# A hybrid decoder block on one core: second-half placement of the attention's values, the fourth output block summed from PSUM, earlier scale row, spread first loads, shifted mixer instructions

## What is computed

```python
mod = c_act @ w_ada[l] + b_ada[l]
shift, scale, gate = jnp.split(mod, 3, axis=-1)
h = rmsnorm(x, g_pre[l]) * (1.0 + scale[:, None]) + shift[:, None]
p = h @ w_in[l]
(a_in, a_g, b_q, b_f, b_i, b_g, c_x, c_b, c_c, c_g,
 d_q, d_k, d_v, d_g, m_g) = jnp.split(p, IN_OFFSETS, axis=-1)
y_pool = pool_mixer(a_in, pool_w[l], pool_scale[l]) * jax.nn.silu(a_g)
y_hgrn = hgrn2_mixer(b_q, b_f, b_i, lower_bounds[l], hgrn_norm[l]) * jax.nn.silu(b_g)
y_conv = short_conv_mixer(c_x, c_b, c_c, conv_w[l]) * jax.nn.silu(c_g)
y_diff = diff_attention(d_q, d_k, d_v, diff_lam[l], diff_norm[l], l) * jax.nn.silu(d_g)
gates = jax.nn.sigmoid(m_g.reshape(B_, T, N_BRANCH, D))
merged = (gates[:, :, 0] * (y_pool @ w_merge_pool[l]) + ...)
out = merged @ w_out[l]
x = x + gate[:, None] * rmsnorm(out, g_post[l])
```

## Time and profile before

| | us |
|---|---|
| median of 3 runs | 2758.57 (2758.25 to 2764.52) |
| the profiled execution | 2759.86 |
| its span, first to last instruction | 2757.8 |
| of it, PE busy | 2355.1 |

### The profile page before, as it was taken

One profiled execution on the slowest core, in us unless ns is written; L12 is line 12 of the kernel. 1 busy time (PEld: TensorE's weight loads), 2 busy tenths in 40 slices (PEclk: granted clock), 3 DMA queues, 4 the chain that ended last, 5 costly groups with the idle time before them and its releaser, 6 DMA issues. The chain is left out here.

```text
span 2757.8 us, 35490 instructions
## 1 busy us (share of the span) xinstructions
PE 2355.1 (85%) x11572; PEld 1913.1 (69%) x11572; DVE 1773.7 (64%) x2868; ACT 1240.0 (45%) x2613; POOL 1231.3 (45%) x1015
## 2 busy tenths in 40 slices
PE   3698868778988889996899999998898965798898
PEld 3576656667776678785787777777677754677676
DVE  6775554544989896544777776688899734453442
ACT  3553444434443444543565656553444333243342
POOL 1442322222866665532333433465767605352543
PEclk9899988989999999998999999999999987899999
DMA  5357533323434334545342332143333356485772
GB/s 209 111 186 228 145 105 90 102 72 116 126 101 122 103 97 128 174 132 151 83 119 77 98 96 83 60 134 117 107 110 123 96 171 159 120 231 143 193 198 73
DMA packets 327262, 350.84 MB, mean 127 GB/s; under 512 B 26416, under 2 KB 244912, under 8 KB 326064
## 3 DMA queue, kind: packets, MB, share of 16 engines
q1 hardware_dynamic: 327088, 348.67, 42.8%
HBM read 242.15 MB, written 106.43 MB: 126 GB/s over the span
## 5 line engine op out<-in xcount | busy, mean ns | idle before, releaser
L1603 PE MATMUL gb<-h_hi,w_hi 128*128 128x512 f32 x1904 | 804.2, 422 | 83.7 <-DVE o L1199 53.4
L1604 PE MATMUL gb<-h_lo,w_hi 128*128 128x512 f32 x1904 | 766.9, 403 | 0.0
L1605 PE MATMUL gb<-h_hi,w_lo 128*128 128x512 f32 x1904 | 766.5, 403 | 0.0
L1191 DVE TENSOR_TENSOR w_lo<-w,w_hi 128x512 fp32r<-128x512 f32 x340 | 333.8, 984 | 337.3 <-ACT w_hi L900 336.5
L1603 PEld LDWEIGHTS gb<-h_hi,w_hi 128*128 128x128 f32 x1904 | 375.0, 197 | 173.7 <-issue 95.9
L1605 PEld LDWEIGHTS gb<-h_hi,w_lo 128*128 128x128 f32 x1904 | 372.4, 196 | 84.1
L1604 PEld LDWEIGHTS gb<-h_lo,w_hi 128*128 128x128 f32 x1904 | 375.4, 197 | 69.8 <-issue 0.2
L916 ACT ACTIVATE o<-gb 128x512 f32<-128x512 f32 x340 | 201.7, 593 | 347.8 <-PE gb L1605 300.1
L764 POOL TENSOR_TENSOR C_prob<-C_prob,C_cf 128x512 f32<-128x512 f32 (+3 forms) x160 | 157.8, 1006 | 383.8 <-DVE C_cf L1299 366.8
L989 ACT ACTIVATE C_prob<-C_sc,C_negm 128x512 f32<-128x512 f32 (+3 forms) x320 | 196.9, 620 | 280.9 <-DVE C_negm L1277 275.0
L748 POOL TENSOR_TENSOR o<-o 128x512 f32<-128x512 f32 x68 | 98.0, 1441 | 409.2 <-ACT o L916 409.1
(11 more groups left out here) (227 smaller groups left out, 4312.2 us busy)
## 6 DMA issues: line engine op xcount, KB each, us to landing
w<-in_w_in_dram SPq DMA_DIRECT2D x136, 512.0 KB, 4.1
gT_scratch<-o SPq DMA_DIRECT2D x128, 256.0 KB, 2.7
D_gate<-gT_scratch SPq DMA_DIRECT2D x32, 1024.0 KB, 9.6
pT_scratch<-o SPq DMA_DIRECT2D x80, 256.0 KB, 3.3
C_qt<-qB_scratch SPq DMA_DIRECT2D x128, 128.0 KB, 2.7
C_ks<-kT_scratch SPq DMA_DIRECT2D x48, 256.0 KB, 4.8
A_x_all<-in_x_dram SPq DMA_DIRECT2D x16, 512.0 KB, 6.5
A_ada<-in_w_ada_dram SPq DMA_DIRECT2D x8, 1024.0 KB, 12.1
```

Of the source, the lines that this page charges most:

```text
L1191: tt(w_lo[n % RING][:, :, :], source(n), w_hi[n % RING][:, :, :].bitcast(F32), ALU.subtract).then_inc(wlo, 1)
L1603: mm(to, hi[:, k, :], h_hi[j][:, k, :], start=(fresh and k == 0), stop=False, skip_group_check=True)
L1604: mm(to, hi[:, k, :], h_lo[j][:, k, :], start=False, stop=False, skip_group_check=True)
L1605: last = mm(to, lo[:, k, :], h_hi[j][:, k, :], start=False, stop=(k == KH - 1), skip_group_check=True)
```

## The change

Eight edits in one:

1. In the first half of the tokens PE takes the transpose back, the values and the transposes of a step half a product after its scores (`attention_behind`), and the transpose back one step earlier (7 instead of 8 steps after the unit's end). DVE's `gate_out` stands ahead of the maxima there, and for the second half ahead of the combination. In the second half ACT copies the turned piece between its two exponentials.
2. The product of j = 4 is no longer copied by ACT and added by POOL: DVE adds bank and block 3 into block 2.
3. The units come in the order k, q, v, v, gate, gate, k, q instead of v, v, gate, gate, k, q, k, q. Attention stands in slots 50 to 109 and 284 to 354.
4. The first loads of attention are issued in five parts, one a slot, from 5 slots ahead on.
5. The row of scales is loaded from slot 6 on, one piece in 3 slots, into one buffer, and ends at slot 35.
6. q is kept in another order in DRAM: 2 stores of 128 rows for a block instead of 4 of 64; its loads read pieces of 512 B instead of 2 KB.
7. Mixers: `shares`'s four scalings go from DVE to ACT; POOL's `same_level` is gone, PE reads the last level from `k_s` and `q_s` themselves.
8. Mixers: transposes from 2 to 4, tokens 3 to 5, norms 11 to 12, root 12 to 13, finish 13 to 14, store 14 to 15; in the second half a block in 12.5 slots, from slot 372.

```diff
-PAIR_COLS = (28, 30, 32, 34, 24, 20, 26, 22) + (4, 6, 8, 0, 2, 10, 12, 14, 16, 18) + tuple(range(36, 68, 2))
+PAIR_COLS = (24, 20, 28, 30, 32, 34, 26, 22) + (4, 6, 8, 0, 2, 10, 12, 14, 16, 18) + tuple(range(36, 68, 2))
+COPIED, SUMMED = (0, 2, 3, 6), (1, 4, 5)
-ATTENTION = ((62, 50), (287, 70))
-MIX_BASE = [130 + 12 * i for i in range(8)] + [374 + 12 * i for i in range(8)]
+ATTENTION = ((50, 60), (284, 71))
+MIX_BASE = [130 + 12 * i for i in range(8)] + [372 + 25 * i // 2 for i in range(8)]
-PREP, ROW = 5, 38
+PREP, ROW = 5, 6
...
+                y = 2 * at0 + s * 2 * span // att_steps[half]
+                att_at[divmod(y, 2)] = half, s
+                att_behind[divmod(y + 1 - half, 2)] = half, s
...
             def load_row(k):
-                if k >= 2:
-                    sp.wait_ge(row_used, k - 1)
-                sp.dma_start(row_in[k % 2], ada_v[:, k, 2 * D:3 * D]).then_inc(row_loaded[k % 2], 16)
+                if k:
+                    sp.wait_ge(row_used, k)
+                else:
+                    sp.wait_ge(mod_summed, 1)
+                sp.dma_start(row_in, ada_v[:, k, 2 * D:3 * D]).then_inc(row_loaded, 16)
...
                 for half in range(HALVES):
-                    if n == ATTENTION[half][0] - (5, 4)[half]:
-                        begin_attention(half)
+                    if 0 <= n - ATTENTION[half][0] + 5 < 5:
+                        begin_attention(half, n - ATTENTION[half][0] + 5)
...
-            def cross(u):
-
-                pool.wait_ge(copied, 5 * u + 4)
-                tt(o[2][:, :], o[2][:, :], o[3][:, :], ALU.add).then_inc(crossed, 1)
...
-                b = {1: 0, 5: 1}[j]
+                b, c = {1: (0, 0), 4: (2, 3), 5: (1, 1)}[j]
                 dve.wait_ge(product_done, n + 1)
-                dve.wait_ge(copied, 5 * u + 1 + b)
-                tt(o[b][:, :], gb[n % 2][:, :], o[b][:, :], ALU.add).then_inc(summed, 1)
+                dve.wait_ge(copied, 4 * u + {1: 1, 4: 3, 5: 2}[j])
+                if j == 4:
+                    output_free(u, b)
+                tt(o[b][:, :], gb[n % 2][:, :], o[c][:, :], ALU.add).then_inc(summed, 1)
...
                 a(f_s[:, :, :], in3[i % 2][:, 2:4, :], ACT.Sigmoid)
-                a(k_s[i % 2][:, :, :], in3[i % 2][:, 2:4, :], ACT.Sigmoid, scale=-1.0)
+                link(a(k_s[i % 2][:, :, :], in3[i % 2][:, 2:4, :], ACT.Sigmoid, scale=-1.0))
+                for t in range(2):
+                    a(f_s[:, t, :], f_s[:, t, :], ACT.Identity, scale=omlb[:, t:t + 1], bias=lb[:, t:t + 1])
+                    a(k_s[i % 2][:, t, :], k_s[i % 2][:, t, :], ACT.Copy, scale=omlb[:, t:t + 1])
...
             def shares(i):
                 dve.wait_ge(sig_ready, i + 1)
-                for t in range(2):
-                    ts(k_s[i % 2][:, t, :], k_s[i % 2][:, t, :], omlb[:, t:t + 1], None, ALU.mult)
-                for t in range(2):
-                    ins = ts(f_s[:, t, :], f_s[:, t, :], omlb[:, t:t + 1], lb[:, t:t + 1], ALU.mult, ALU.add)
-                link(ins)
...
+            def attention_behind(half, s):
+                i = None if half else finished(half, s, ON)
+                if i is not None:
+                    turn_back(i)
                 z = piece(half, s, VALUES)
...
-                i = mix_step(n, 11)
+                i = mix_step(n, 12)
                 if i is not None:
                     norms(i)
-                i = mix_step(n, 2)
+                i = mix_step(n, 4)
                 if i is not None:
                     transposes(i)
```

More of the change, by code:

```diff
@@ L1526, in _ @@
                             distances(ending[z])
+                    i = finished(half, s, GATE) if half else None
+                    if i is not None:
+                        gate_out(i)
                     z = piece(half, s, COMBINE)
@@ L1529, in _ @@
                         combine(z)
-                    i = finished(half, s, GATE)
-                    if i is not None:
-                        gate_out(i)
                 for half in range(HALVES):
```

223 lines of the change are left out of this document (113 added, 110 removed).

## The result

| | us |
|---|---|
| median before (4 runs beside it) | 2758.41 (2757.41 to 2764.52) |
| median after (4 runs) | 2598.84 (2593.64 to 2601.82) |
| ratio, with its 95% interval | 0.9415 (0.9395 to 0.9435) |
| profiled execution after, its span | 2601.82, 2600.0 |

A forecast was written before the change was run, and what follows sets the result against it. PE, busy 85% of the span, was taken as the bound, losing time to waits and low clock. Terms -76 - 20 - 15 + 5 - 40 - 2 = -148 took 2759.9 to 2612, so 2611 for the median; range 2575 to 2690.

The forecast's parts named there:

- The signs that it named: Waits, clock and DVE share expected if right, such as first attention's clock 0.95 or more, mixers' DVE under 90%.
- the wait only changes its name: Rival, first half's attention: PE waits for `C_on` as before for `C_y_out`, the 76 us are gone; 2687, chance 0.05.
- the stores stay the bound: Rival where q, k and first loads share a queue: 35 us stay, start costs 10 more; 2656, chance 0.10.
- the better case: Rival: first half's waits and clock loss go entirely and the mixers give 60 us; 2562, chance 0.06.
- The attention's order, -76: First half's attention: -66.6 of waits, -36.7 of clock, +16 at transpose back, +11 small waits; bounds -95 and -40.
- The fourth block, 0 in the attention: DVE gains 68 additions, 46.6 us; hidden outside the mixers, +9.6 us of DVE per half in them.
- the new add hides in its idle time: Outside the mixers, DVE is busy 52 to 72% of the time, so its added fourth-block work was taken as hidden.
- Units, row, first loads, -20 and -15, start +5: Before first attention -20 (-5 to -30); second half's first scores -15 (-8 to -20); start +5 (0 to +15).
- Mixers, -40: Both halves' mixers: lighter DVE and later norms and transposes give -20 a half; bounds 0 and -60 in all.
- The norms come a product later: Mixers: norms move 2.7 to 3.9 us later, against waits for the state of 3.7 mean, 5.4 at most.
- ACT's order in the second half, -2: Second half's attention: values get their input sooner, the second exponential comes later; -2 us, bounds -8 and +8.

The follow-up runs named there:

- the burst in the changed kernel: Changed kernel with the 21 first loads of the second half's attention issued in one slot, 4 ahead, as before: 2605.77 us, ratio 0.9453.
- the root first: Changed kernel with the norms' root (Ln and Exp) ahead of the sigmoids in ACT's slot, not behind them: 2577.54 us, ratio 0.9336.
- two attempts: Changed kernel, root ahead of sigmoids; first half's transpose back ahead of the next step's scores (2577.11 us), or last in its own step (2573.31 us).

## Why the prediction was right, and where it was not

**Sign and size.** -148 forecast, -158 in the profiled executions. The signs that it named came: no wait for `C_y_out`, clock 0.98 in the first attention, 2.7 us for the state, 3.0 us at the second half's first scores, DVE at 85% in the mixers, 60.7 us of waits for DVE's additions. None of the rivals came whole. Of "the wait only changes its name" 25.8 us did, a mean of 0.92, where 0.5 was taken; 2 of the 28 waits passed 2 us. Of "the stores stay the bound" the part on the start did. That the sum came so close is in part luck: the attention's order and the mixers gave 26 and 16 us less than forecast, the start lost 9 more, and the fourth block gave some 33 for which the sum had nothing. Two details don't follow from the working: half the way from 2611 to the better case is 2586, not the range's 2575, and a load of q is 128 KB in the profile, not 64 (its median time to landing went from 2.7 to 2.9 us, so the 512-byte pieces cost little, as was taken).

**The attention's order, -76.** Undoing it gives back 50 us. I counted all of the 66.6 us and all of the clock's 36.7 as this one edit's; with the old order back the waits are 57.2 us and the clock is 0.91, not 0.87. The stretch got even shorter, by 83.6 us, but if the parts add, 13.4 of it are the fourth block's, 3.9 the units', and 10.2 the wait at product 60, which belongs to the first loads or the row. Some 6 are left (83.6 - 50.2 - 13.4 - 3.9 - 10.2), which no run separates: the steps now have 60 slots instead of 50.

**The fourth block, 0 in the attention and +9.6 us of DVE in each half's mixers.** The step that failed is "the new add hides in its idle time": it priced only what DVE gains. It is worth some 33 us by the ratios. In the profiled execution it was 42: 13 and 16 in the two attentions, 6 and 9 in the mixers, -0.5 in 14 to 50, some -1 elsewhere. 685 ns was right for the addition, but not that nothing else moves: ACT loses a copy among the exponentials, and `w_lo` gives back 43.8 of the 46.8 us. The 984 ns that the prediction took as the neighbouring price was a mean of 689 ns alone and 1216 beside POOL. The rule on the two SBUF inputs stood in the prediction for the instruction that comes; it bears as much on the 476 that stay, once a POOL instruction beside them goes.

**Units, row, first loads, -20 and -15, start +5.** In products 0 to 34 13.6 us were lost, not 5, of them 1.9 in the first five, where kernels that should agree differ by up to 2.8. The mechanism was named (the row's first load and k's stores in one queue behind x) but the sum was too small: the row's additions cost nothing, the wait at product 9 is 4.7 us, the new units 2.5 at most, and DVE's fourth sum 5.0, which was not priced here at all. From 34 to 50 18.0 came back, 6.0 by the units, and the 10.2 us at product 60 went too; no run says how much of this is the row's and how much the first loads'. The second half's first loads: their wait went from 16.5 to 3.0 us. The new units alone bring it to 11.2 and win 4.1 us in products 222 to 354; the burst in the changed kernel costs 7.2 there. Together that is 11, so -15 was some 4 too much.

**Mixers, -40.** Measured -24.1, and -40.6 with the root first (14.9 and 1.6 more). By part: scalings -11.3, fourth block -14.4 (perhaps too high by a fifth), root's place +16.5, which leaves -14.9 for the other offsets, the wider spacing and POOL's `same_level`, not separated. The failed step is "The norms come a product later": it priced the wait that this cures, and not in which slot of ACT the root then stands, what is there already, and which tables are loaded. The change says root 12 to 13, and with 12 slots a block 13 is 1. I asked that question of queues (SP, DVE) and not of this one.

**ACT's order in the second half, -2.** Measured -3.4 in the stretch, within the intervals of the medians. The second attention as a whole fell by 42.4: 15.9 by the fourth block, 3.4 by this, 13.5 by the first scores' wait. Ten us of it stay open. q's new order in DRAM was not undone alone.

## What to carry over

Before moving an instruction by a slot, list what else its engine has in the new slot, modulo the period of the loop, and which activation table is then loaded; the mean busy share of the engine says nothing on that. Price an operation that is removed from a third engine by what it slowed beside it, too: `w_lo` got 116 ns shorter in the mean, 340 times, with nothing done to it. A mean like its 984 ns can hide two prices; look at single instructions, with and without company. And when a wait only changes its name in two attempts, look at what its engine does ahead of the late instruction, not at the instruction.

## What the runs showed of the hardware

- Ln and Exp behind a sigmoid loaded a table each, 1283 ns and 1283 ns, though the same kernel runs both from one loaded table where it asks for that ahead (line 1158: one load, 1283 ns, for Ln and the Exps behind it). The Trainium skill (ScalarE: Activation LUTs, Table sets: the hidden batching unit) says that one set holds both; the trace shows that this helps only where that set is loaded ahead of them.
- Behind a table load of 1.28 us at 760.52 the activation started at 761.81, so on ACT the whole price here is 1.28 us.
- `w_lo`, 128x512 with two SBUF inputs, took 690 ns alone and 1180 in the mean beside a POOL instruction (after), 1366 beside POOL's sum of the same size (fourth block back on POOL). DVE's addition of a PSUM bank took 687 ns alone and 685 beside POOL.
- 57.2 us of PE's waits in 15 pieces went with a mean granted clock of 0.91 in the first half's attention, 25.8 us in 28 pieces with 0.98. A busy PE took 201 ns an instruction in the one (294.41 over 1466) and 189 in the other (276.42 over 1466). The granted clock fell to its lower level 14 times in the one stretch, 64.9 us in all, and twice in the other, 10.2 us; in the kernel before 16 times, 102.4 us.
